# Hybrid decoder layer on one core: norms by square root and reciprocal, head squares summed on VectorE, two final scalings on GpSimd

## What is computed

```python
def rms_norm(x, g):
    xf = x.astype(jnp.float32)
    y = xf * lax.rsqrt(jnp.mean(xf * xf, axis=-1, keepdims=True) + RMS_EPS)
    return (y * g.astype(jnp.float32)).astype(x.dtype)
...
    m = g[:, :, 0] * (o_nsa @ w_o_nsa) + g[:, :, 1] * (o_rwkv @ w_o_rwkv) + g[:, :, 2] * (o_mem @ w_o_mem)
    x = x + m @ w_out
    hf = rms_norm(x, ffn_norm)
    return x + (jax.nn.silu(hf @ w_gate) * (hf @ w_up)) @ w_down
...
    y_prompt = rms_norm(xp, final_norm)
    y_sample = rms_norm(xs, final_norm)
```

## Time and profile before

| what | us |
|---|---|
| median of 3 runs (range) | 1673.18 (1670.27 to 1676.35) |
| the profiled execution | 1671.82 |
| its span in the trace | 1670.0 |
| TensorE busy in it | 1600.3 (96%) |
| VectorE, ScalarE, GpSimd busy | 454.0, 383.8, 103.4 |

### The profile page before, as it was taken

How to read it: one execution, slowest core, us unless ns; L and a number is a source line. 1 busy time by engine, 2 the same in 40 slices (tenths; PEclk the granted TensorE clock), 3 DMA queues, 4 the chain that set the end, 5 groups by cost and what they waited for, 6 DMA issues and landing times.

```text
span 1670.0 us, 30995 instructions
## 1 busy us (share of the span) xinstructions
PE 1600.3 (96%) x13440; PEld 1247.5 (75%) x13440; DVE 454.0 (27%) x915; ACT 383.8 (23%) x734; POOL 103.4 (6%) x186
## 2 busy tenths in 40 slices
PE   6999999999999999998999789999999999999997
PEld 5888578877777766775667558878788888888886
DVE  1112004523323335414774432221111111110002
ACT  3011145212222214215776431001100000000002
POOL 0000000010100102204001110000000000000000
PEclk9999999999999999999999999999999999999999
DMA  5222362320111226446002873312122122222221
GB/s 207 75 76 63 101 210 97 97 79 22 41 41 41 78 61 208 163 135 205 7 2 76 285 274 125 129 64 75 63 76 76 63 75 75 65 74 76 70 70 54
DMA packets 56445, 161.79 MB, mean 97 GB/s; under 512 B 7136, under 2 KB 20544, under 8 KB 55136
## 3 DMA queue, kind: packets, MB, share of 16 engines
q1 hardware_dynamic: 47744, 120.87, 22.3%
q0 software_dynamic: 7136, 35.73, 6.3%
q10 hardware_dynamic: 1440, 3.33, 0.6%
HBM read 141.91 MB, written 22.15 MB: 98 GB/s over the span
## 4 chain that ended last, share of the span: by engine, by line
PE 90%; DVE 2%; SPq 2%; issue 2%; ACT 2%; DMA 1%; ACTq 0%; DVEq 0%
PE acc L1643 19%; PE acc L935 18%; PE acc L884 9%; PE acc L1667 8%; PE acc L1601 7%; PE acc L1623 4%; PE acc L921 2%; PE acc L1030 2%; PE acc L1371 2%; PE acc L909 2%; PE acc L1395 2%; PE acc L1384 2%; PE acc L1044 1%; SPq L630 1%; PE acc L1002 1%
## 5 line engine op out<-in xcount | busy, mean ns | idle before, releaser
L935 PE MATMUL acc<-sb_work,sb_ring 128*128 128x272 f32 x1280 | 334.2, 404 | 1.0 <-ACT sb_work L1750 1.0
L1643 PE MATMUL acc<-sb_work,sb_ring 128*128 128x272 f32 x1408 | 322.8, 392 | 0.0
L1643 PEld LDWEIGHTS acc<-sb_work,sb_ring 128*128 128x128 f32 x1408 | 267.5, 190 | 55.1
L935 PEld LDWEIGHTS acc<-sb_work,sb_ring 128*128 128x128 f32 x1280 | 231.9, 190 | 57.4 <-issue 10.5
L884 PE MATMUL acc<-sb_work,sb_ring 128*128 128x272 f32 x640 | 148.8, 396 | 3.8 <-DVE sb_work L2073 3.8
L884 PEld LDWEIGHTS acc<-sb_work,sb_ring 128*128 128x128 f32 x640 | 122.6, 192 | 29.8 <-issue 4.2
L1667 PE MATMUL acc<-sb_work,sb_ring 128*128 128x272 f32 x616 | 141.3, 392 | 0.0
L1667 PEld LDWEIGHTS acc<-sb_work,sb_ring 128*128 128x128 f32 x616 | 117.0, 190 | 24.1
L2038 ACT ACTIVATE sb_work<-sb_work (+1 forms) x22 | 14.4, 657 | 277.4 <-DVE sb_work L2511 277.4
L1750 ACT ACTIVATE sb_work<-acc 128x272 f32<-128x272 f32 x80 | 31.5, 395 | 162.2 <-PE acc L935 154.5
L2487 DVE TENSOR_TENSOR sb_work<-acc,sb_work 128x544 f32<-128x544 f32 (+1 forms) x17 | 11.8, 692 | 191.8 <-PE acc L1667 132.8
(11 more groups left out here) (376 smaller groups left out, 1893.3 us busy)
## 6 DMA issues: line engine op xcount, KB each, us to landing
sb_ring<-w_stream SPq DMA_DIRECT2D x158, 512.0 KB, 3.5
sb_work<-pages SPq DMA_DIRECT2D x64, 192.0 KB, 3.8
branch_gates<-sb_work SPq DMA_DIRECT2D x24, 272.0 KB, 4.4
sb_work<-branch_gates POOLq DMA_DIRECT2D x8, 816.0 KB, 14.5
sb_work<-mem_kT SPq DMA_DIRECT2D x8, 512.0 KB, 6.5
sb_work<-mem_v SPq DMA_DIRECT2D x8, 512.0 KB, 8.8
query_features<-sb_work SPq DMA_DIRECT2D x10, 272.0 KB, 4.3
sb_work<-x_T ACTq DMA_DIRECT2D x8, 272.0 KB, 4.6
```

The source lines that it names most:

```text
L935: mm = pe.matmul(acc[3][:, half, 0:HALF_T], fill_w[0][:, k, :], hT[:, k, half * HALF_T:(half + 1) * HALF_T], start=k == 0, stop=k == KT - 1)
L1643: mm = pe.matmul(acc[2 * x + n % 2][:, b, 0:HALF_T], w[:, k, :], hT[:, k, b * HALF_T:(b + 1) * HALF_T], start=k == 0, stop=k == KT - 1)
```

## The change

It has three parts.

- **Head norm.** ScalarE begins with a square root of 128 columns of ones. The squares of tile 0 go to a new buffer `h_total`; VectorE adds the other seven to it one after another, and TensorE sums `h_total` once (two products, 4 records, in place of 32). ScalarE may run up to two squares ahead of VectorE's sum.
- **All four norms.** `ones_h` and `ones` hold 1/D in place of 1. In place of logarithm and exponential, ScalarE takes a square root (`Sqrt`) and VectorE takes `reciprocal` of it in place: of 544 columns for head and FFN norm, 256 for the memory norm, 272 for each half at the end. A square root of one element is put behind the last FFN tile, ahead of the squares.
- **The end.** ScalarE multiplies tiles 3 and 5 of `x1T` by the final weight once their squares are made. GpSimd multiplies these two tiles by `rms`, half by half, while VectorE scales six tiles in place of eight. The order in which SP stores pairs stays; its waits count VectorE's and GpSimd's tiles apart.

Semaphores are reused under new names: `h_added` is `sq_added`, `pf_done` is `h_squared`, `rms_root` is `h_rms`.

```diff
+        h_total = region(None, T)
...
+        h_added, pf_done, rms_root, SQ, PF, RR = sq_added, h_squared, h_rms, KT - 1, 2 * KT, 2
...
-                    sp.wait_ge(hf_done, KT + b * KT + j + 2)
+                    sp.wait_ge(hf_done, KT + 2 + 6 * b + (2, 3, 4, 6)[j // 2])
+                    if j in (2, 4):
+                        sp.wait_ge(pf_done, PF + 2 * b + j // 2)
...
+            for b in range(2):
+                cols = slice(b * HALF_T, (b + 1) * HALF_T)
+                pool.wait_ge(hf_done, KT + 2)
+                pool.wait_ge(rms_inv, b + 2)
+                for j in (3, 5):
+                    pool.tensor_tensor(x1T[:, j, cols], x1T[:, j, cols], rms[:, cols], ALU.mult).then_inc(pf_done, 1)
...
-            for k in range(KT):
-                pe.wait_ge(h_squared, k + 1)
-                for b in range(2):
-                    mm = pe.matmul(acc[3][:, b, 0:HALF_T], ones_h, h_square[:, k % 2, b * HALF_T:(b + 1) * HALF_T],
-                                   start=k == 0, stop=k == KT - 1)
-                mm.then_inc(h_sum, 1)
+            pe.wait_ge(h_added, KT - 1)
+            for b in range(2):
+                mm = pe.matmul(acc[3][:, b, 0:HALF_T], ones_h, h_total[:, b * HALF_T:(b + 1) * HALF_T], start=True, stop=True)
+            mm.then_inc(h_sum, 1)
...
+            own(act.activation(h_total[:, 0:P], ones_h, ACT.Sqrt))
             for k in range(KT):
...
-                if k >= 2:
-                    act.wait_ge(h_sum, k - 1)
-                act.activation(h_square[:, k % 2, :], xT[:, k, :], ACT.Square).then_inc(h_squared, 1)
-            act.wait_ge(h_sum, KT)
-            own(act.activation(h2(h_scale), acc[3][:, :, 0:HALF_T], ACT.Ln, scale=1.0 / D, bias=stat[:, 20:21]))
-            act.activation(h_scale, h_scale, ACT.Exp, scale=-0.5).then_inc(h_rms, 1)
+                if k >= 3:
+                    act.wait_ge(h_added, k - 2)
+                act.activation(h_square[:, k % 2, :] if k else h_total, xT[:, k, :], ACT.Square).then_inc(h_squared, 1)
+            act.wait_ge(h_sum, 1)
+            act.activation(h2(h_scale), acc[3][:, :, 0:HALF_T], ACT.Sqrt, bias=stat[:, 20:21]).then_inc(h_rms, 1)
...
-                    own(act.activation(mem_scale, acc[3][:, 0, 0:MEM_T], ACT.Ln, scale=1.0 / D, bias=stat[:, 20:21]))
-                    act.activation(mem_scale, mem_scale, ACT.Exp, scale=-0.5).then_inc(h_rms, 1)
+                    act.activation(mem_scale, acc[3][:, 0, 0:MEM_T], ACT.Sqrt, bias=stat[:, 20:21]).then_inc(h_rms, 1)
...
-            own(act.activation(h2(rms), acc[3][:, :, 0:HALF_T], ACT.Ln, scale=1.0 / D, bias=stat[:, 20:21]))
-            act.activation(rms, rms, ACT.Exp, scale=-0.5).then_inc(rms_inv, 1)
+            act.activation(h2(rms), acc[3][:, :, 0:HALF_T], ACT.Sqrt, bias=stat[:, 20:21]).then_inc(rms_root, 1)
...
+            own(act.activation(stat[:, 0:1], stat[:, 1:2], ACT.Sqrt))
             for j in range(KT - 1):
                 act.wait_ge(x1_added, KT + j + 1)
                 square(j, KT)
+                if j in (3, 5):
+                    act.wait_ge(sqT_made, KT + j + 1)
+                    act.activation(x1T[:, j, :], x1T[:, j, :], ACT.Copy, scale=v("final", j)).then_inc(hf_done, 1)
...
-                own(act.activation(rms[:, cols], acc[3][:, b, 0:HALF_T], ACT.Ln, scale=1.0 / D, bias=stat[:, 20:21]))
-                act.activation(rms[:, cols], rms[:, cols], ACT.Exp, scale=-0.5).then_inc(rms_inv, 1)
-                if b == 0:
-                    act.activation(stat[:, 0:1], stat[:, 1:2], ACT.Ln)
+                act.activation(rms[:, cols], acc[3][:, b, 0:HALF_T], ACT.Sqrt, bias=stat[:, 20:21]).then_inc(rms_root, 1)
...
+            for k in range(1, KT):
+                dve.wait_ge(h_squared, k + 1)
+                if k >= 2:
+                    dve.wait_ge(h_added, k - 1)
+                dve.tensor_tensor(h_total, h_total, h_square[:, k % 2, :], ALU.add).then_inc(h_added, 1)
             dve.wait_ge(x_in[1], 16 * KT // 2)
             dve.wait_ge(h_rms, 1)
+            own(dve.reciprocal(h_scale, h_scale))
...
+                    own(dve.reciprocal(mem_scale, mem_scale))
...
+            dve.wait_ge(rms_root, RR + 1)
+            dve.reciprocal(rms, rms).then_inc(rms_inv, 1)
             dve.wait_ge(rms_inv, 1)
...
+                dve.wait_ge(rms_root, RR + 2 + b)
+                dve.reciprocal(rms[:, cols], rms[:, cols]).then_inc(rms_inv, 1)
                 dve.wait_ge(rms_inv, b + 2)
                 for j in range(KT):
-                    dve.scalar_tensor_tensor(x1T[:, j, cols], x1T[:, j, cols], v("final", j), rms[:, cols],
-                                             ALU.mult, ALU.mult).then_inc(hf_done, 1)
+                    if j not in (3, 5):
+                        dve.scalar_tensor_tensor(x1T[:, j, cols], x1T[:, j, cols], v("final", j), rms[:, cols],
+                                                 ALU.mult, ALU.mult).then_inc(hf_done, 1)
```

More of the change, by code:

```diff
@@ L889, in _ @@
                     pe.wait_ge(h_squared, 2 * KT)
+                    pe.wait_ge(h_rms, 1)
                     for k in range(KT):
@@ L1625, in _ @@
                 mm.then_inc(slot_used, 1)
-            pe.wait_ge(sq_added, KT - 2)
+            pe.wait_ge(sq_added, SQ + KT - 2)
             square_sum(0)
@@ L1680, in _ @@
                     if b == 0 and k == FFT // 2:
-                        pe.wait_ge(sq_added, 2 * (KT - 2))
+                        pe.wait_ge(sq_added, SQ + 2 * (KT - 2))
                         square_sum(0)
@@ L1720, in _ @@
                 if n == N_RW - 4:
-                    act.wait_ge(h_sum, KT + 1)
-                    own(act.activation(mem_scale, acc[3][:, 0, 0:MEM_T], ACT.Ln, scale=1.0 / D, bias=stat[:, 20:21]))
-                    act.activation(mem_scale, mem_scale, ACT.Exp, scale=-0.5).then_inc(h_rms, 1)
-            act.wait_ge(h_sum, KT + 2)
+                    act.wait_ge(h_sum, 1 + 1)
+                    act.activation(mem_scale, acc[3][:, 0, 0:MEM_T], ACT.Sqrt, bias=stat[:, 20:21]).then_inc(h_rms, 1)
+            act.wait_ge(h_sum, 1 + 2)
             act.activation(h2(gates_sT[0:36]), acc[2][0:36, :, 0:HALF_T], ACT.Sigmoid).then_inc(mem_done, 1)
@@ L1734, in _ @@
                    .then_inc(mem_done, 1)
-            act.wait_ge(h_sum, KT + 3)
+            act.wait_ge(h_sum, 1 + 3)
             act.activation(gates_tm[:, 0:QT, :], acc[2][:, 1, HALF_T:HALF_T + 36 * QT].rearrange("p (n c) -> p n c", n=QT), ACT.Copy)\
@@ L2022, in square @@
                 if j >= 2:
-                    act.wait_ge(sq_added, done * (KT - 2) // KT + j - 1)
+                    act.wait_ge(sq_added, SQ + done * (KT - 2) // KT + j - 1)
                 act.activation(sqT[:, min(j, 1), cols], x1T[:, j, cols], ACT.Square).then_inc(sqT_made, 1)
@@ L2064, in _ @@
             dve.memset(stat[:, 21:22], GN_EPS)
-            dve.memset(ones_h, 1.0).then_inc(means, 1)
+            dve.memset(ones_h, 1.0 / D).then_inc(means, 1)
             dve.wait_ge(x_in[0], 16 * (KT // 2 + 1))
@@ L2467, in _ @@
             dve.wait_ge(ms_done, MS + 2)
-            own(dve.memset(ones, 1.0))
+            own(dve.memset(ones, 1.0 / D))
             for m in range(KT):
@@ L2491, in add_square @@
                 if j >= 2:
-                    dve.wait_ge(sq_added, done * (KT - 2) // KT + j - 1)
+                    dve.wait_ge(sq_added, SQ + done * (KT - 2) // KT + j - 1)
                 dve.tensor_tensor(sqT[:, 0, :], sqT[:, 0, :], sqT[:, 1, :], ALU.add).then_inc(sq_added, 1)
```

## The result

The changed kernel takes 1680.47 us in the median of 18 runs (1677.19 to 1688.38); beside it the kernel before takes 1672.45 us (18 runs, 1668.61 to 1676.35). The ratio is 1.0049, 95% interval 1.004 to 1.0058: **8.0 us slower**. The forecast was 1673.6 us, no measurable change, with 1669.0 to 1677.5 as its range, so both the direction and the size were missed.

A forecast was written before the change was run, and what follows sets the result against it. TensorE, 90% of the chain, bounds the kernel, so only start and end can move: -0.6 + 1.0 = +0.4 us, which from the median of 1673.18 gives 1673.6 us; range 1669.0 to 1677.5.

The forecast's parts named there:

- three signs that the prediction gave for being wrong: Long reciprocals below 1 us, the first weight tile at low clock throughout, or VectorE's FFN work waiting for `rms`.
- The last store follows the last scaling as before: At the end: GpSimd's two tiles, 0.6 to 0.8 us each, finish before VectorE's six, so nothing is added.
- An edit on ScalarE, VectorE or GpSimd can only move the time where TensorE stands still: Whole kernel: only the start, up to 23.73 us, and the end, after 1658.84 us, can change.
- Price of a reciprocal: VectorE, all norms: 7.2 ns a column, so 4.1 us for 544 columns, 2.1 for 272, 2.0 for 256.
- The rival of a cheap reciprocal: Start and end: a long reciprocal costs what an add does, sum -6.2 us, 1667.0 us; chance 0.07.
- Head norm: At the start: first weight tile begins at 22.25 us in place of 23.73, 1.5 us earlier.
- The clock: First weight tile: TensorE starts at low clock for 5.2 us after resting, 0.9 us later.
- The late clock of the rival: First weight tile: low clock lasts 6.7 us, +1.7 us there, 1674.4 us in all; chance 0.20, including 0.03 for the whole tile.
- Memory and FFN norm: Middle norms: no time change, the FFN reciprocal ending 2.6 us before VectorE needs it.
- The end, up to the last scaling: After TensorE's last product: last scaling ends about 9.4 us behind it in place of 8.4, 1.0 us later.
- the rival of a harmless GpSimd: At the end: GpSimd doesn't slow VectorE's scalings, sum -1.4 us, 1671.8 us; chance 0.17.
- The rival of loads that hold ScalarE twice as long: Two table loads removed from the path each held ScalarE another 1.28 us, sum -2.2, 1671.4 us; chance 0.04 including others.

The follow-up runs named there:

- e5: e4 plus 56 semaphore increments that nobody waits for at the head of TensorE's queue: 1670.57 us, ratio 0.9992 to the kernel before.
- e4: Kernel before with only the head norm's squares summed on VectorE, logarithm and exponential kept: 1675.35 us, ratio 1.0016.
- e1: Changed kernel without GpSimd's part, VectorE scaling all eight tiles of each half: 1675.56 us, ratio 1.0017 to the kernel before.
- e3: Kernel before with square root and reciprocal alone at all four norms, head's squares still summed on TensorE: 1674.2 us, ratio 1.001.
- e6: Changed kernel plus 56 semaphore increments at the head of TensorE's queue: 1676.45 us, ratio 1.0026 to the kernel before.
- e9: e4 with the 56 instructions filled up by 12 semaphore increments and 11 unused products on TensorE: 1668.19 us, ratio 0.9973 to the kernel before.
- e2: Kernel before with GpSimd's part alone, logarithm and exponential kept: 1677.0 us, ratio 1.0024.
- e8: Kernel before plus one unused 8-column memset on GpSimd after VectorE's last scaling: 1678.25 us, ratio 1.0037.

## What was right and what was wrong, step by step

By ratios, times 1672.5 us, the change comes apart like this. Each row adds one thing to the row above.

| kernel | ratio | what is added | us |
|---|---|---|---|
| before | 1 | | |
| e5 | 0.9992 | head's squares summed on VectorE, TensorE's stream as long as before | -1.3 |
| e4 | 1.0016 | 56 instructions fewer in TensorE's stream | +4.0 |
| e1 | 1.0017 | square root and reciprocal | +0.2 |
| after | 1.0049 | tiles 3 and 5 on GpSimd | +5.4 |

The interval of each ratio is about 0.001, 1.7 us, each way, so that of a difference between two rows is over 2 us: +4.0 and +5.4 are clear of it, -1.3 and +0.2 are not. Alone, square root and reciprocal cost 2 us (e3); beside the new head sum no cost of them can be told. With the two terms that the forecast put at nothing it comes out: 0.4 + 3.7 (GpSimd's close) + 4.0 (the stream) = 8.1 us, where 8.0 were measured; the 3.7 is read from single executions, so so close a match is partly luck. None of the three signs that the prediction gave for being wrong appeared, since all three watched other steps.

**"The last store follows the last scaling as before": wrong.** With the stream's 4.0 us this is the step that failed: 3.7 of GpSimd's 5.4 us. It looked at when GpSimd's two tiles are ready (1670.38, before VectorE's 1671.92, right, though they took 0.95 to 1.01 us each and not 0.6 to 0.8) and not at what GpSimd has still to do when its queue ends. The kernel's time ends with the last engine, and GpSimd needs 8.0 us for it. A sign of it stood in the kernel before: GpSimd's last work was at 1052 us, so its close had never been on the path, and I had noted that GpSimd had nothing to do in the last 600 us without asking what that had spared.

**"An edit on ScalarE, VectorE or GpSimd can only move the time where TensorE stands still": it doesn't cover this change.** The change also takes 56 instructions out of TensorE's queue, and the sum priced them at nothing outside the head. They move the later pauses to other code: about 4 us (e4 against e5, the change against e6). That the place in the stream costs this is shown; what makes TensorE pause there isn't. The pauses could be read in the kernel before, up to 4.26 us with "issue" as the only reason, though not what governs them.

**Price of a reciprocal: near.** VectorE's groups of the kernel after, busy us and mean ns:

```profile
L2555 DVE RECIPROCAL sb_work<-sb_work 128x272 f32<-128x272 f32 x2 | 3.7, 1853 | 8.3 <-ACT sb_work L2065 8.3
L2085 DVE RECIPROCAL sb_work<-sb_work 128x544 f32<-128x544 f32 x1 | 3.6, 3553 | 3.2 <-ACT sb_work L1719 3.2
...
L2108 DVE RECIPROCAL sb_work<-sb_work 128x256 f32<-128x256 f32 x1 | 1.8, 1753 | 2.2 <-ACT sb_work L1731 2.2
```

3.55, 1.85 and 1.75 us, where 4.1, 2.1 and 2.0 were taken; the slope is (3553 - 1853) / 272 = 6.25 ns a column, not 7.2. The rival of a cheap reciprocal falls. The 8.3 ns worked out from the Trainium skill's repeat count of 8 (VectorE: DVE Perf Modes, First, the fixed hardware budget) is 33% above it; that a reciprocal is dear was right.

**Head norm: the gain was 0.85 us, not 1.5.** Squares began at 8.26, not 7.5: the square root's small start ended at 7.68, 0.2 late, and the data of this execution came at 8.2. The adds took 5.71 us for seven, a step of 0.83 and not 0.76, since each waits for its own result as well as for a square; they end at 15.21, not 14.1. TensorE's four records 2.15 (2.3 taken), square root 0.71. The shorter reciprocal gave 0.55 back. One remark of the prediction doesn't give its own 1.5: not 5.6 us go but 18.70 - 14.1 = 4.6 and load and exponential 2.0, so 6.6, and 6.6 - 5.1 is 1.5.

**The clock: near, as far as five traces tell.** In the profiled execution of the change the weight tile took 32.31 - 22.88 = 9.43 us, against 9.35: +0.1, not +0.9. The other four with the sum on VectorE and a TensorE that rests took 9.6 (e4), 10.1 (e1), 10.2 (e5) and 10.7 (e6), so +0.1 to +1.3 in all, and +0.9 lies within. That the start as a whole came out at -0.8, near the forecast's -0.6, is luck of this execution: the gain was 0.65 too high and the clock's loss 0.8 too high. The windows (columns as for e9) show a granted 1.00 here, where the earlier trace rows had 0.50, but the first products, in ns minimum/median/maximum in the second block, last as long as those from rest in the earlier trace rows:

```profile
22.90:25.00 2.10, 2.10 (x5) 1.64 (x6) 2.10 (x4) 0.00 (x0) 0.00 (x0) 1.00 0.67 271
25.00:28.40 3.40, 3.40 (x14) 2.70 (x13) 2.85 (x5) 0.00 (x0) 0.00 (x0) 1.00 0.00 0
```

```profile
L892 PE MATMUL acc<-sb_work,sb_ring x5: 661/661/793, 22.9 to 24.8; 128*128 128x272 f32 x5
```

From 26.8 us on every product lasts 392 ns again, so the low pace kept on for at most 3.9 us, not 5.2. The late clock of the rival, +1.7, came in none of the five.

**Memory and FFN norm: nothing, as said.** The FFN's reciprocal ends at 1181.38 us, and VectorE's next work comes 3.2 us later, where 2.6 were forecast:

```profile
1177.83 3.55 DVE L2520 RECIPROCAL sb_work<-sb_work 128x544 f32<-128x544 f32 x1 [2.94 <-ACT sb_work L2039]
```

**The end, up to the last scaling: right.** 9.4 us behind TensorE's last product were forecast, 9.5 came. GpSimd does slow VectorE: six scalings take 3.57 us beside it, 3.45 were forecast, and eight take 3.39 alone. So two tiles fewer brought nothing; the pair in the earlier trace rows was the right price, and the rival of a harmless GpSimd falls. TensorE's two sums of half 1 took 1.19 us, at the low clock, where e2 and e8 show 0.73. So the 9.5 is near partly because errors cancel: the reciprocals were 0.25 us shorter each, these sums 0.46 and each half's scalings 0.12 longer.

**Table loads: as their rows.** The rival of loads that hold ScalarE twice as long falls by the kernel before itself: the logarithm ends at 20.70 us, the load begins at 20.73 and ends at 22.01, and VectorE starts at 22.79, one exponential of 0.7 later. There is no room for a second 1.28. This rival's time was also added up wrongly: 1673.2 - 2.2 is 1671.0, not 1671.4.

## What to carry to other kernels

Every engine has a close after its last instruction, and on an engine that was idle for long it hides under the others' work. Before such an engine gets the last bit of work, find out from a trace in which it finishes last how long its close takes, and count that. And this kernel, bound by TensorE and with a long unrolled stream, has pauses that depend on how many instructions stand ahead: when an edit adds or removes some of them, try the same edit with the number kept and shifted, before its few microseconds are put down to its arithmetic.
